# Two reorderings in a fused two-block transformer kernel: which side of a branch TensorE meets first, and where VectorE rotates the retention keys

## The reference

```python
x = token_mixer(...) ; x = x + post_norm(...)           # block 1, a gated recurrence
h = moe_ffn(h, ...)    # 64 experts, 8 for each token, 1024 -> 2*256 -> 1024, and one shared expert
# block 2: mixer_block, then squared_relu_mlp
proj = xn @ w_in                                        # q_a k_a v_a q_r k_r v_r g_r gate_a gate_r
y_a  = sliding_window_sink_attention(q_a, k_a, v_a)     # 8 heads of 64, blocks of 128 tokens
q_r  = apply_rope(q_r, cos, sin)                        # retention, 4 heads of 128
k_r  = apply_rope(k_r, cos, sin) * RET_KEY_DIM ** -0.5
ret  = chunkwise_retention(q_r, k_r, v_r)
```

## Time and profile before

| | us |
|---|---|
| three runs | 2194.71, 2198.81, 2199.42 |
| median | 2198.81 |
| profiled execution, its own time | 2194.71 |
| its span (first to last instruction) | 2192.8 |
| PE busy | 2091.7 (95%) |
| DVE, ACT, POOL busy | 1216.5, 961.3, 240.6 |

### The profile page before, as it was taken

One profiled execution on the slowest core, in us unless ns is written; L12 is line 12 of the kernel. 1 busy time (PEld: TensorE's weight loads), 2 busy tenths in 40 slices (PEclk: granted clock), 3 DMA queues, 4 the chain that ended last, 5 costly groups with the idle time before them and its releaser, 6 DMA issues.

```text
span 2192.8 us, 32763 instructions
## 1 busy us (share of the span) xinstructions
PE 2091.7 (95%) x12066; PEld 1686.6 (77%) x12067; DVE 1216.5 (55%) x2089; ACT 961.3 (44%) x1349; POOL 240.6 (11%) x217
## 2 busy tenths in 40 slices
PE   7998989998999999999989999999999999999998
PEld 3787977788567667776666666988888898899898
DVE  3858577446566556666656657456653244423433
ACT  4337365233366546665556654334332224312322
POOL 0004023000122222222223220000000000000000
PEclk9999989999999999999999999999999999999999
DMA  9831111263589778999988985311122213222221
GB/s 353 285 106 59 47 51 58 78 258 121 233 304 334 275 243 323 335 346 330 336 289 313 346 282 195 127 60 58 39 77 96 96 58 125 97 96 81 94 97 58
DMA packets 76666, 392.51 MB, mean 179 GB/s; under 512 B 16321, under 2 KB 32833, under 8 KB 46049
## 3 DMA queue, kind: packets, MB, share of 16 engines
q1 hardware_dynamic: 57506, 357.33, 43.8%
q0 software_dynamic: 19008, 33.22, 6.2%
HBM read 384.03 MB, written 42.48 MB: 195 GB/s over the span
## 4 chain that ended last, share of the span: by engine, by line
PE 55%; DMA 11%; DVE 4%; issue 3%; ACT 2%; POOLq 0%; DVEq 0%; SPq 0%; ACTq 0%; POOL 0%
PE bank L3293 16%; DMA ffn_sums<-moe_work 10%; PE bank L2232 5%; PE bank L2976 3%; PE bank L2978 3%; PE bank L2977 3%; PE bank L2210 3%; PE bank L2214 3%; PE bank L2213 3%; PE bank L2961 2%; PE bank L2963 2%; PE bank L2962 2%; PE bank L2198 1%; PE bank L2169 1%; DVE moe_gu_rest L1996 1%
## 5 line engine op out<-in xcount | busy, mean ns | idle before, releaser
L2578 DVE TENSOR_TENSOR b_w_rest<-ring,b_w_high 128x2048 fp32r<-128x2048 f32 x63 | 144.4, 2292 | 180.0 <-ACT b_w_high L2573 179.7
L2232 PE MATMUL bank<-moe_work 128*128 128x512 f32 x512 | 236.1, 602 | 1.5 <-issue 1.3
L2210 PE MATMUL bank<-moe_gu_high,moe_x_high 128*128 128x512 f32 x512 | 207.0, 404 | 9.9 <-DVE moe_x_rest L2004 4.1
L1996 DVE TENSOR_TENSOR moe_gu_rest<-moe_work,moe_gu_high 128x2048 fp32r<-128x2048 f32 x64 | 143.8, 2289 | 125.7 <-ACT moe_gu_high L1750 125.7
L1996 DVE TENSOR_TENSOR moe_gu_rest<-ring,moe_gu_high 128x2048 fp32r<-128x2048 f32 x64 | 143.8, 2289 | 123.8 <-ACT moe_gu_high L1750 123.8
L2214 PE MATMUL bank<-moe_gu_high,moe_x_rest 128*128 128x512 f32 x512 | 201.3, 393 | 0.0
L2213 PE MATMUL bank<-moe_gu_rest,moe_x_high 128*128 128x512 f32 x512 | 200.7, 392 | 0.0
L2573 ACT ACTIVATE b_w_high<-ring 128x2048 fp32r<-128x2048 f32 x63 | 120.5, 1913 | 177.4 <-PE bank L3293 126.7
L2977 PE MATMUL bank<-b_w_rest,b_h_high 128*128 128x256 f32 x608 | 171.7, 282 | 0.0
L1771 ACT ACTIVATE moe_work<-bank,moe_work 128x512 f32<-128x512 f32 x124 | 78.6, 685 | 198.4 <-PE bank L2232 101.6
L2232 PEld LDWEIGHTS bank<-moe_work 128*128 128x128 f32 x512 | 92.1, 190 | 91.9 <-issue 90.7
(11 more groups left out here) (505 smaller groups left out, 5006.8 us busy)
## 6 DMA issues: line engine op xcount, KB each, us to landing
ring<-in_stream_dram SPq DMA_DIRECT2D x105, 1024.0 KB, 4.8
moe_work<-in_experts_dram SPq DMA_DIRECT2D x32, 2048.0 KB
moe_work<-in_experts_dram SPq DMA_DIRECT2D x64, 1024.0 KB
ring<-in_experts_dram SPq DMA_DIRECT2D x32, 2048.0 KB
X<-in_stream_dram SPq DMA_DIRECT2D x16, 512.0 KB, 7.8
mixer_work<-in_stream_dram SPq DMA_DIRECT2D x16, 512.0 KB, 6.4
X<-in_x_dram SPq DMA_DIRECT2D x8, 512.0 KB, 8.8
ffn_sums<-mixer_work SPq DMA_DIRECT2D x8, 512.0 KB, 4.9
```

Source lines behind the costliest of these rows:

```text
L1996: v.tensor_tensor(WL[o % 4][h], guslot[o % 4][:, HALF * h:HALF * (h + 1)], WH[o % 2][h], ALU.subtract).then_inc(s["w_rest"], 1)
L2210: first = mm(banks[2][:, :], xh[:, k, :], wh[h][:, c], start=(k == 0), stop=False)
L2232: product = mm(banks[bank + j][:, :], HDT[o % 2][:, k, :], w[:, k, 512 * j:512 * (j + 1)], start=(k == 0), stop=(k == 1))
L2578: nc.vector.tensor_tensor(WL[u % FEED], raw(u), high_at(u), ALU.subtract).then_inc(s["w_rest"], 1)
```

## The change

In `woven_block` the test for an ordinary expert moves behind the code for further blocks. In block 2 all four key tiles are rotated at n = 2, at the place where the queries are rotated at n = 1.

```diff
     def woven_block(eng, i, u, done, first, later, ordinary):
         count = eng.value_load(CNT[0:1, index(i, u)])
-        with eng.If(count <= P):
-            ordinary(i, u)
         with eng.If(count > P):
             first(i, u, eng.snap(done[0]), eng.snap(done[1][u % 2]))
...
+        with eng.If(count <= P):
+            ordinary(i, u)
...
-            if n == NT - 1:
-                dve.wait_ge(*item_read(("kr", 1, 1)))
-                turned_keys(0)
-                turned_keys(1)
             dve.wait_ge(s["es_ready"], n + 1)
...
             w_rest(dve, (6, 8, 10, 11)[n])
-            if n == 1:
-                dve.wait_ge(*item_read(("qr", 1, 1)))
+            if n in (1, 2):
+                dst, kind, name = ((QR, "qr", "rot_q"), (KR, "kr", "rot_k"))[n - 1]
+                dve.wait_ge(*item_read((kind, 1, 1)))
                 for t in range(NT):
-                    rotate(grid(QR[:, t, :], 4), ...)
-            if n == NT - 1:
-                turned_keys(2)
-                turned_keys(3)
+                    rotate(grid(dst[:, t, :], 4), ...)
             if n < 2:
                 w_rest(dve, (7, 9)[n])
             dve.wait_ge(s["av_high"], n + 1)
```

More of the change, by code:

```diff
@@ L2787, in dve_part @@
         win = con("win")
-        def turned_keys(t):
-            rotate(grid(KR[:, t, :], 4), grid(con("kcos"), 4)[:, t, :], grid(con("ksin"), 4)[:, t, :], "rot_k", t + 1)
         for n in range(NT):
@@ L2817, in dve_part @@
             w_rest(dve, (6, 8, 10, 11)[n])
-            if n == 1:
-                dve.wait_ge(*item_read(("qr", 1, 1)))
+            if n in (1, 2):
+                dst, kind, name = ((QR, "qr", "rot_q"), (KR, "kr", "rot_k"))[n - 1]
+                dve.wait_ge(*item_read((kind, 1, 1)))
                 for t in range(NT):
-                    rotate(grid(QR[:, t, :], 4), grid(con("qcos"), 4)[:, t, :], grid(con("qsin"), 4)[:, t, :], "rot_q", t + 1)
-            if n == NT - 1:
-                turned_keys(2)
-                turned_keys(3)
+                    rotate(grid(dst[:, t, :], 4), grid(con(kind[0] + "cos"), 4)[:, t, :],
+                           grid(con(kind[0] + "sin"), 4)[:, t, :], name, t + 1)
             if n < 2:
```

## The result

| | before | after |
|---|---|---|
| median | 2198.36 us (4 runs) | 2213.06 us (4 runs, 2209.75 to 2216.72) |
| ratio | | 1.0068, 95% interval 1.0047 to 1.009 |
| profiled execution, own time / span | 2194.71 / 2192.8 | 2212.31 / 2210.6 |

The change costs 14.7 us. The forecast was 2204.2 us, and the result lies outside its range as well. Slower was right, the size was not.

A forecast was written before the change was run, and what follows sets the result against it. PE, busy 95% of the span, was taken as the bound. Stall +5.0, clock +1.5 and branch -1.1 summed to +5.4 us, on the median of 2198.8 giving 2204.2 us, range 2198 to 2209.

The forecast's parts named there:

- Keys, the stall: Block 2 attention, n = 3: PE's second half of the scores waits for DVE's key rotation, +5.0 us, bounds 0 and 9.6.
- Keys, the clock: Behind the new gap in the n = 3 scores: granted clock drops, +1.5 us, bounds 0 and 3.0.
- the kinder rival: Stall at n = 3 stays, but clock stays up and late branches are hidden: +2.5 to +3.9 us; chance 0.33.
- Branch, the later passes: Experts after the first pass: about 0.27 us of sequencer time per ordinary expert moves from behind `turn_hidden` to ahead of `down`.
- a late place: One of three experts where `turn_hidden` came late and PE was empty before `gate_up`: 0.27 us saved each, 0.8 together.
- a further block: Three experts with a further block get one more taken branch before the next `gate_up`: 3 x 0.27 = 0.8 us lost.
- the common expert: About two thirds of the 61 ordinary experts: 2.1 us of queued work covers the branch ahead of `down`, no cost.
- the fifteen with little cover: Experts from 988 to 1102 and 1258 to 1303 us, cover about 0.3 us ahead of `down`: 0, upper end 4 us.
- Branch, the first pass: Two long branches, at 618.1 and 651.3 us, move ahead of `down`: 0.5 saved each, bounds 1.9 saved to 1.6 lost.
- The second is covered by 2.1 us: The 1445 ns branch at 651.3 us, moved ahead of `down`, is hidden by 2.1 us of queued work: 0.5 saved.
- 2.9 + 0.1 less 2.1 leaves 0.9 of its 1.4: The 2878 ns branch at 618.1 us, moved ahead of `down`, is only partly covered by queued work: 0.5 us saved.
- the branch costs where `down` is late: Rival: fifteen experts with little cover pay 0.27 us each, or more fetches come late: +4 us more, 2208.2; chance 0.12.

The follow-up runs named there:

- 2: Only the keys part of the change (all four key tiles at n = 2), branch as before, against the kernel before: 1.0031, +6.7 us.
- 9: The whole change, with gate-up weights of experts 4 to 11 released at the end of `gate_up`, not its start, against the kernel before: 1.003, +6.6 us.
- 3: The branch part alone, with the loop's gate-up weights released at the end of `gate_up`, not its start, against the kernel before: 0.9999.
- 5: The branch part alone, with only the gate-up weights of experts 4 to 11 released at the end of `gate_up`, against the kernel before: 1.0002.
- 1: Only the branch part of the change, keys as before, against the kernel before: 1.0034, +7.5 us.
- 6: The branch part, with 128 spare semaphore increments at the start of PE's program moving its later code to higher addresses, against the kernel before: 1.0075, increments not hidden.
- 10: The kernel before, with only the gate-up weights of experts 4 to 11 released at the end of `gate_up`, against the kernel before unedited: 1.0009.
- 4: The kernel before, with all the loop's gate-up weights released at the end of `gate_up`, against the kernel before unedited: 0.9984, 3.4 us faster.

## Why the prediction was wrong

- **Keys, the stall: right.** 5.13 us where 5.0 were worked out, by the mechanism named: DVE's queue ahead of the score read, 4.4 us of it in DVE's hole.
- **Keys, the clock: right in kind, mis-sized.** The term was 1.5 us (one stretch of 3.4), it measured 3.15 to 3.5 by the traces: one stretch of 10.2 us. I took the length from a drop that followed 3.8 us of empty PE; 5.1 us of empty PE gave three times that. It exceeds the bound of 3.0 a little. By time the part is +6.7 us against a forecast of 6.5, and that agreement is partly luck: the traces of after, 2 and 9 give 8.2 to 8.7 us at this place and take 0.9 to 1.0 back at 1633, which I had not forecast.
- **Clock, the evidence for the kinder rival: one execution's luck.** I held against the drop that PE's 2.1 us of idle time at 1369 to 1371 cost no clock. The same gap of 2.05 us was followed by 3.4 or 6.8 us at half clock in 11 of the 13 other traces.
- **Branch, the later passes: right.** 0.31 saved at a late place, 0.32 lost behind a further block, nothing in the common expert, and no cost that shows in the fifteen with little cover; with the fetches out of the way (3, 5) the part costs nothing.
- **Branch, the first pass: this step failed.** "The second is covered by 2.1 us" and "2.9 + 0.1 less 2.1 leaves 0.9 of its 1.4" take the 2878 and 1445 ns as the length of a job that moves along with the branch. They were the rest of a wait for a fetch. The fetch moves behind the weights, so the end of the jump stays where the weights put it, and the branch that is met 3.6 and 3.8 us earlier against them lasts 3.5 and 3.7 us longer. The cover of 2.1 us was there and was overrun: PE is empty for 4.29 and 3.19 us, 7.5 in all, against 1.5 before (1.19 and 0.33; the 1.9 that I counted as to be saved was PEld's), 6.0 more. The low clock behind both gaps (3.4 us each, the first from 619.9) came on top: together after loses 8.8 us from the first expert to the ninth. The term was forecast at 1.0 saved, with bounds of 1.9 saved and 1.6 lost; by time the whole part is 7.5 us lost against 1.1 saved.
- The trace of before held the warning: its 2878 ns branch comes at the end of a stretch with the DMA engines at 0.98 (615 to 618), with no packet of q8 in it. The rival "the branch costs where `down` is late" names late fetches ahead of `down`, but as more fetches of a fixed price, 4 us in all; it was the same two, each with a longer wait.
- What the order of the branches is worth depends on the layout and the weights: against the kernel before it loses 8.8 (after) and 11.3 us (1) in the first passes with the weights early, 2.6 with the code moved (6), and wins 2.3 to 2.4 with the weights late (3, 5, 9).
- The Trainium skill ("Runtime: NRT & Kernel Launch", section "Instruction fetch mechanics") says that a taken branch whose target is outside the window of fetched instructions stalls the sequencer for a fetch. The first pass agrees, with 6.4 and 5.2 us. The 50 branches of the later passes last 216 ns or less, and no packet of q8 moves there.

Open: when exactly a fetch is asked for, and so which jump, or which straight piece of code (6, 10), of a given layout is hit. Experiment 6 shows that it moves with the code's place, and 4 that it may come ahead of the jump.

## What to carry to other kernels

A duration in a trace is a price only if nothing else sets its end: before moving a long wait, see what it ends with (here an instruction fetch that came late in a burst of weights); if something else sets the end, the wait only grows when it is met earlier. Code that is met for the first time, jump or not, had better not be met while megabytes are on their way to the same core, and the first pass over a loop has costs that a median over its passes doesn't show. A stall of PE of some us is to be priced with the clock that follows, read from more than one trace, and spare matrix work in the gap buys the clock back, not the stall.

## What the runs showed of the hardware

- An instruction fetch (one packet of 16 KB, queue q8) that met 3 MB of weights moved 7.9 to 8.0 us after the last weight issue at the first place and 5.9 to 6.6 at the second, in four kernels (before, after, 1 and 2). The branch that waited ended 2.3 to 2.4 us behind the packet, and also in 6, where the DMA engines stood nearly idle by then (0.06 in 608.5:610). So a jump lasted 6.4 us, and 0.42 where it was met 2.4 us behind its packet (3).
- Straight code waits as well: 1.78 us in the middle of `gate_up` (10) and 2.25 us in the middle of `down` (6), each ended 2.3 to 2.5 us behind a packet of q8.
- Between 678 and 1285 us the kernel before has no fetch on q8: the code of four experts, further block included, stays on the core, and a taken branch is 208 ns.
- 5.13 us of empty PE brought the granted clock to 0.50 for 10.2 us, three times in three kernels (after, 2, 9). Shorter gaps are less certain: 4.2 to 4.3 us gave 3.4 us (after) and 6.8 (1), 3.2 and 3.8 us gave 3.4 and 6.8 (the same two), and one and the same gap of 2.05 us in front of block 2's first transposes (L2619) gave none in 3 traces of 14, 3.4 us in 5 and 6.8 in 6.
- Gaps of 1.50 and 1.38 us close together were followed by 3.4 or 6.8 us at half clock in all twelve traces that have them, and by none in the two with 22 transposes in them.
